# One decoder step on one core: final norm and output by token tile, expert rows gathered raw and scaled afterwards, first slots picked earlier

## The reference, cut to what matters

```python
def _rmsnorm(x, g):
    xf = x.astype(jnp.float32)
    xf = xf * lax.rsqrt(jnp.mean(xf * xf, axis=-1, keepdims=True) + EPS)
    return (xf * g.astype(jnp.float32)).astype(x.dtype)

def _moe(h, w_router, b_router, w_g, w_u, w_d):       # h = _rmsnorm(x, g_ffn)
    logits = (h @ w_router).astype(jnp.float32) + b_router
    probs = jax.nn.softmax(logits, axis=-1)
    topv, topi = lax.top_k(probs, 2)
    topv = topv / jnp.sum(topv, axis=-1, keepdims=True)
    gates = ...                                       # (token, expert), two entries per token
    for e in range(8):
        y = y + gates[..., e:e + 1] * _swiglu(h, w_g[e], w_u[e], w_d[e])
...
x = x + _moe(...)
y = _rmsnorm(x, g_final)
```

## Time and profile before

| | us |
|---|---|
| three runs | 2106.89, 2109.68, 2114.77 (median 2109.68) |
| the profiled execution | 2111.83 |
| its span, first to last instruction | 2110.1 |
| one turn, from transposes to transposes | 75.8 |

### The profile page before, as it was taken

How to read it: one execution, slowest core, us unless ns; L and a number is a source line. 1 busy time by engine, 2 the same in 40 slices (tenths; PEclk the granted TensorE clock), 3 DMA queues, 4 the chain that set the end, 5 groups by cost and what they waited for, 6 DMA issues and landing times.

```text
span 2110.1 us, 35352 instructions
## 1 busy us (share of the span) xinstructions
PE 1886.1 (89%) x14245; PEld 1796.3 (85%) x14245; DVE 1192.0 (56%) x1787; ACT 874.6 (41%) x1305; POOL 186.5 (9%) x226
## 2 busy tenths in 40 slices
PE   4999999877999999969999897877999999999983
PEld 4988987776999999969889787767999999999983
DVE  3765444366333333346654344566787788788872
ACT  5542133614322222155321335244565555555542
POOL 2022200002000000010321000000000000000020
PEclk9999998798999999989999888988999999999995
DMA  4211021014933233222111210235777777778773
GB/s 147 82 51 42 21 72 55 26 64 166 373 94 105 74 96 108 76 55 83 41 41 31 72 45 26 64 109 157 249 265 231 235 262 244 242 248 260 226 219 86
DMA packets 74993, 271.20 MB, mean 129 GB/s; under 512 B 13728, under 2 KB 16176, under 8 KB 72832
## 3 DMA queue, kind: packets, MB, share of 16 engines
q1 hardware_dynamic: 63328, 219.77, 32.9%
q0 software_dynamic: 11552, 49.81, 7.1%
HBM read 234.22 MB, written 35.32 MB: 128 GB/s over the span
## 4 chain that ended last, share of the span: by engine, by line
PE 73%; DVE 14%; ACT 7%; issue 4%; DMA 2%; POOL 1%; DVEq 0%; POOLq 0%; SPq 0%; ACTq 0%
PE ps L633 71%; DVE sb_w_lo L2292 4%; DVE sb_s L1652 2%; ACT sb_s L1165 2%; DVE sb_s L1660 1%; DVE sb_afg L2328 1%; ACT sb_w_hi L1153 1%; ACT L1165 1%; DVE sb_h_lo L1652 1%; DVE sb_w_lo L1643 1%; PE ps L1093 1%; DMA sb_w_raw<-in_wd 1%; PE ps L750 1%; ACT sb_ga L1165 1%; POOL sb_y L491 0%
## 5 line engine op out<-in xcount | busy, mean ns | idle before, releaser
L633 PE MATMUL ps<-sb_h_hi,sb_w_hi 128*128 128x260 f32 x1952 | 578.7, 296 | 31.4 <-DVE sb_h_lo L1652 25.8
L633 PE MATMUL ps<-sb_h_hi,sb_w_lo 128*128 128x260 f32 x1952 | 563.2, 289 | 0.0
L633 PE MATMUL ps<-sb_h_lo,sb_w_hi 128*128 128x260 f32 x1952 | 562.5, 288 | 0.0
L633 PEld LDWEIGHTS ps<-sb_h_hi,sb_w_hi 128*128 128x128 f32 x1952 | 381.0, 195 | 46.6 <-issue 28.3
L1153 ACT ACTIVATE sb_w_hi<-sb_w_raw 128x1024 fp32r<-128x1024 f32 (+2 forms) x144 | 153.9, 1070 | 602.0 <-PE ps L633 601.9
L633 PE MATMUL ps<-sb_hg,sb_w_hi 128*128 128x320 f32 x1408 | 377.9, 353 | 15.3 <-DVE sb_w_lo L2292 8.5
L633 PEld LDWEIGHTS ps<-sb_h_lo,sb_w_hi 128*128 128x128 f32 x1952 | 380.7, 195 | 3.3 <-issue 3.1
L1582 ACT ACTIVATE sb_w_hi<-sb_w_raw 128x1024 fp32r<-128x1024 f32 (+1 forms) x241 | 276.1, 1146 | 251.3 <-PE ps L633 236.5
L633 PEld LDWEIGHTS ps<-sb_h_hi,sb_w_lo 128*128 128x128 f32 x1952 | 380.0, 195 | 0.0
L1643 DVE TENSOR_TENSOR sb_w_lo<-sb_w_raw,sb_w_hi 128x1024 fp32r<-128x1024 f32 (+2 forms) x144 | 181.6, 1262 | 324.6 <-ACT sb_w_hi L1153 324.6
L633 PE MATMUL ps<-sb_hg,sb_w_lo 128*128 128x160 f32 x1408 | 331.9, 236 | 0.0
(11 more groups left out here) (260 smaller groups left out, 2384.5 us busy)
## 6 DMA issues: line engine op xcount, KB each, us to landing
sb_w_raw<-in_wgu SPq DMA_DIRECT2D x223, 512.0 KB, 4.0
sb_w_raw<-in_wd SPq DMA_DIRECT2D x80, 704.0 KB, 6.8
sb_w_raw<-in_wz SPq DMA_DIRECT2D x62, 512.0 KB, 3.5
rows_y<-sb_s POOLq DMA_DIRECT2D x16, 1280.0 KB, 29.7
sb_w_raw<-in_wo SPq DMA_DIRECT2D x16, 384.0 KB, 3.1
rows_y<-sb_x POOLq DMA_DIRECT2D x16, 320.0 KB, 5.5
sb_x<-in_xT SPq DMA_DIRECT2D x8, 260.0 KB, 5.5
rows_h<-sb_rows POOLq DMA_DIRECT2D x5, 416.0 KB, 5.2
```

What stands on the lines that cost most here:

```text
L633: return pe.matmul(out, lhsT, rhs, start=start, stop=stop, skip_group_check=True)
```

## The change

1. Router: `HTK` goes; GpSimd stores the unscaled rows `XTK` to `HX`. `RST` is now Sqrt on ScalarE and a reciprocal on VectorE. Its two parts go into `GE` as two more columns, so that `key` and `slots` also gather the norm factor of each slot, into `GCN[..., 1]`. The last weight split of the output projection moves behind the last `tokens` copy.
2. Turns: `turned` scales the gathered rows first, half s = 0 on ScalarE (80x1024), half s = 1 on VectorE (80x1024); TensorE's transposes wait for both instead of for the gather.
3. First slots: `select(0, 0)`, `key(0)`, `slots(0)` and `fetch(0, 0)` come ahead of the turn count, the register reads and `addresses`.
4. End: one semaphore for each gathered tile of `R2`; add, square with its own sum, square root, reciprocal, scaling of `XTK`, eight transposes and the multiplication by `g_final` run tile by tile, each engine's steps interleaved by program order. `DIAG` and the separate sums go.
5. Some semaphores are merged (`silu_g` and `ssilu_a` into `glu_a` and so on), with their counts moved accordingly.

```diff
@@ pool @@
+            pool.wait_ge(sem["xtk_v"], KT)
             for i in range(NT):
-                pool.wait_ge(sem["htk_a"], i + 1)
-                pool.dma_start(HX[i * TT:(i + 1) * TT, :], HTK[0:TT, i, :])...
+                pool.dma_start(HX[i * TT:(i + 1) * TT, :], XTK[0:TT, i, :])...
...
+            fetch(0, 0)
             pool.wait_ge(sem["turns_v"], 1)
             final = pool.value_load(...)
-            fetch(0, 0)
@@ pe, turned @@
-                pe.wait_ge(sem["hrow_d"], it * 32 + 32)
+                pe.wait_ge(sem["hsc_a"], it + 1)
+                pe.wait_ge(sem["hsc_v"], it + 1)
@@ pe, end @@
-                pe.wait_ge(sem["final_v"], 3 * NT + i + 1)
+                pe.wait_ge(sem["xtk_v"], KT + i + 1)
...
-                    last = mm(PS[...], XTK[0:TT, i, k * P:(k + 1) * P], DIAG[0:TT, i, :])
+                    last = pe.transpose(PS[...], XTK[0:TT, i, k * P:(k + 1) * P], ident[0:TT, 0:TT])
@@ act, router @@
-                ex(RST[0:TT, :], PS[0:TT, 0, 0:NT], ACT.Ln, scale=1.0 / D, bias=EPSC[0:TT, :])
-                own(act, "a_ord")
-                ex(RST[0:TT, :], RST[0:TT, :], ACT.Exp, "rs_a", scale=-0.5)
-                act.wait_ge(sem["xtk_v"], KT)
...
-                    ex(HTK[0:TT, i, :], XTK[0:TT, i, :], ACT.Copy, "htk_a", scale=RST[0:TT, i:i + 1])
...
+                ex(RST[0:TT, :], PS[0:TT, 0, 0:NT], ACT.Sqrt, "rs_a", scale=1.0 / D, bias=EPSC[0:TT, :])
+                act.wait_ge(sem["sel_v"], 1)
+                ex(RTK[:, 4, :, :], RTK[:, 4, :, :], ACT.Exp, "rexp_a")
@@ act, turned @@
+                act.wait_ge(sem["hrow_d"], it * 32 + 32)
+                act.wait_ge(sem["gc_v"], it + 1)
+                ex(HROW[0:ST_, 0, :], HROW[0:ST_, 0, :], ACT.Copy, "hsc_a", scale=GCN[0:ST_, 0, 1:2])
@@ act, end @@
-                inc(act.activation(R2[0:TT, i, :], XTK[0:TT, i, :], ACT.Square), "final_a")
...
+                inc(act.activation(R2[0:TT, i, :], XTK[0:TT, i, :], ACT.Square, accum_out=SS[0:TT, i:i + 1]), "final_a")
+                own(act, "final_a")
+                ex(RST[0:TT, i:i + 1], SS[0:TT, i:i + 1], ACT.Sqrt, "final_a", scale=1.0 / D, bias=EPSC[0:TT, :])
+                if i >= 2:
+                    spread(i - 2)
+            spread(NT - 2)
+            spread(NT - 1)
@@ dve, o2 and order @@
-                if m % OQ == OQ - 1:
+                if m % OQ == OQ - 1 and not (l and m == OU - 1):
                     split_at(UB[l] + ZU + OU + m // OQ + 2)
...
+                        if l and arg == OU:
+                            tokens(OU - 1)
                         sq(2 * l + 1, arg - 1)
                     elif name == "rnf":
                         if l:
-                            tokens(OU - 1)
+                            split_at(UB[l] + ZU + OW + 1)
@@ dve, turned @@
+                dve.wait_ge(sem["hrow_d"], it * 32 + 32)
+                dve.wait_ge(sem["gc_v"], it + 1)
+                ts(HROW[0:ST_, 1, :], HROW[0:ST_, 1, :], GCN[0:ST_, 1, 1:2], ALU.mult, name="hsc_v")
@@ dve, first turn @@
+            select(0, 0)
+            slots(0)
+            turns()
+            addresses()
+            taken(0)
             final = dve.value_load(...)
-            select(0, 0)
-            slots(0)
             turned(0)
@@ dve, end @@
+            def scaled(i):
+                dve.wait_ge(sem["final_a"], 2 * i + 2)
+                inc(dve.reciprocal(RST[0:TT, i:i + 1], RST[0:TT, i:i + 1]), "v_ord")
+                done()
+                ts(XTK[0:TT, i, :], XTK[0:TT, i, :], RST[0:TT, i:i + 1], ALU.mult, name="xtk_v")
...
             for i in range(NT):
-                if i == 0:
-                    dve.wait_ge(sem["r2_d"], 16 * NT)
+                dve.wait_ge(sem[f"r2_d{i}"], 16)
                 dve.wait_ge(sem["final_v"], i + 1)
                 inc(dve.tensor_tensor(XTK[0:TT, i, :], XTK[0:TT, i, :], R2[0:TT, i, :], ALU.add), "final_v")
-            for i in range(NT):
-                sums(i)
...
+                if i >= 1:
+                    scaled(i - 1)
+                if i >= 2:
+                    spread(i - 2)
+            scaled(NT - 1)
+            spread(NT - 2)
+            spread(NT - 1)
```

More of the change, by code:

```diff
@@ L211, in build @@
         new(*[f"w_raw{i}" for i in range(RAW_E)])
-        new("load_x0", "load_x1", "ssum_v", "xtk_p", "xtk_v", "htk_a", "idx_v", "hrow_d", "yrow_a", "ys_d",
-            "beat_g", "final_v", "final_a", "y_stored", "r1_d", "r2_d", "slot_v")
+        new("load_x0", "load_x1", "ssum_v", "xtk_p", "xtk_v", "hsc_a", "hsc_v", "hrow_d", "yrow_a", "ys_d",
+            "beat_g", "final_v", "final_a", "y_stored", "r1_d", "slot_v", "yo_v", "yo_a")
+        new(*[f"r2_d{i}" for i in range(NT)])
         count = dict.fromkeys(sem, 0)
@@ L623, in _ @@
             step(final * 2 + 2)
-            collect(R1, 0, "r1_d")
+            for i in range(NT):
+                collect(R1, 0, i, "r1_d")
             put(final, final * 2 + 3)
@@ L627, in _ @@
             step(final * 2 + 4)
-            collect(R2, 1, "r2_d")
+            for i in range(NT):
+                collect(R2, 1, i, f"r2_d{i}")
         @block.tensor
@@ L740, in l2 @@
                 if i:
[L741 removed]
+                    W(pe, "rs2_a", l, i)
                 else:
@@ L1072, in key @@
                     for i in range(NT):
-                        last = mm(PS[0:ST_, 6, 4 * s:4 * s + 4], SelG[0:TT, i, s * ST_:(s + 1) * ST_], GE[0:TT, i, :],
+                        last = mm(PS[0:ST_, 6, 6 * s:6 * s + 6], SelG[0:TT, i, s * ST_:(s + 1) * ST_], GE[0:TT, i, :],
                                   i == 0, i == NT - 1)
@@ L1303, in l2 @@
                 W(act, "l2_p", l, i + 1)
-                ex(ls[i].rearrange("p (a b) -> p a b", a=4), PS[:, 4:8, 0:HALF], ACT.Ln, "ln2_a", bias=EPSC)
+                ex(ls[i].rearrange("p (a b) -> p a b", a=4), PS[:, 4:8, 0:HALF], ACT.Ln, "rs2_a", bias=EPSC)
                 if i:
-                    own(act, "ln2_a")
+                    own(act, "rs2_a")
                     for i in range(2):
@@ L1482, in sc @@
                                           ACT.Copy)
-                inc(last, "stail_a")
+                inc(last, "tail_a")
             def yhi(l, part):
@@ L1557, in group @@
                         split_next(2 * f)
-                        ex(halves(SG[:, f % 2, :]), slot(1 - f % 2), ACT.Silu, "silu_g")
+                        ex(halves(SG[:, f % 2, :]), slot(1 - f % 2), ACT.Silu, "glu_a")
                         split_next(2 * f + 1)
@@ L1588, in turned, with spread @@
                     ex(HG[:, k, 0, :], PS[:, k // 3, (k % 3) * CAP:(k % 3 + 1) * CAP], ACT.Copy, "hgh_a", scale=par[:, g:g + 1])
+            def spread(i):
+                act.wait_ge(sem["xtk_p"], KT + i + 1)
+                for k in range(4, KT):
+                    a = PAR["g_final"][0] + k
+                    last = act.activation(YO[:, k, i * TT:(i + 1) * TT], PS[:, 2 * (i % 4) + 1, (k % 4) * TT:(k % 4 + 1) * TT],
+                                          ACT.Copy, scale=par[:, a:a + 1])
+                inc(last, "yo_a")
             def rows_out(it):
@@ L1623, in _ @@
                 act.wait_ge(sem["final_v"], NT + i + 1)
-                inc(act.activation(R2[0:TT, i, :], XTK[0:TT, i, :], ACT.Square), "final_a")
[L1625 to L1631, removed]
-                    a = PAR["g_final"][0] + k
-                    last = act.activation(YO[:, k, i * TT:(i + 1) * TT], PS[:, 2 * (i % 4) + 1, (k % 4) * TT:(k % 4 + 1) * TT],
-                                          ACT.Copy, scale=par[:, a:a + 1])
-                inc(last, "final_a")
+                inc(act.activation(R2[0:TT, i, :], XTK[0:TT, i, :], ACT.Square, accum_out=SS[0:TT, i:i + 1]), "final_a")
[5 more added lines that the diff above has]
+            spread(NT - 1)
         @block.vector
@@ L2306, in select, with taken @@
                 cp(GE[0:TT, :, 0:2], g.bitcast(F32), "selg_v")
-                if isinstance(it, int) and it == 0:
-                    addresses()
+                if not (isinstance(it, int) and it == 0):
+                    taken(e)
+            def taken(e):
                 dve.tensor_scalar(expert(KEY[0:TT, :, :], e), expert(KEY[0:TT, :, :], e), float(-CAP), None, ALU.add)
```

123 lines of the change are left out of this document (58 added, 65 removed).

## The result

The changed kernel takes 2132.57 us (median of 4 runs, 2128.96 to 2133.07), the kernel before, timed beside it, 2111.59 us: ratio 1.0093, 95% interval 1.0070 to 1.0116. It is slower by 21.0 us on the medians; the forecast was 2114 us, no change that can be told.

The account below looks back on a forecast made before the run. TensorE, busy 89% of the span, was taken as the bound. End -24.2, router -5.3 and turns +33.4 sum to +3.9 us on the median 2109.7: 2113.6, say 2114 us, range 2101 to 2128.

Parts of the forecast that it names:

- So a turn costs 2.85 + 7/8 x 1.7 = 4.35: Each turn: 2.85 us TensorE stall, plus 1.7 us lost at half clock behind seven of eight gaps.
- The end: Last norm, tile by tile from the first landing, its last spread ending near 2082.1 instead of 2106.3: -24.2 us.
- rival C: At the end, Square and Sqrt need different tables, two loads per tile on ScalarE: total +12.6, 2122 us; chance 0.06.
- The router: Before the first transposes: gather 6.4 us earlier, store late next, less 1.12 us for scaling the rows: -5.3 us.
- The stall of a turn: At m = 2, TensorE waits for VectorE's scaling behind its split of m = 1: 2.85 us with pipe refilling.
- Rival D: In the turns, the scaling never holds TensorE up and costs nothing: total -29.5, 2080 us; chance 0.06.
- rival A: In the turns, the clock holds through the new gaps: turns cost 22.9, total -6.6, 2103 us; chance 0.14.
- The clock's price: In seven turns, work lost at half clock: 1.7 us per 3.4 us stretch, behind seven of eight gaps.
- The last turn: TensorE waits 4.3 us behind a late weight load, but the old 1.99 us gap and half clock are taken up: net 2.9.
- Rival B: In each turn, half clock lasts two stretches, gap and transposes lying in both: turns 48, total +19, 2128 us; chance 0.14.
- the turns: All eight turns' cost from the scaling ahead of the transposes: 7 x 4.35 + 2.9 = +33.4 us.

Follow-up runs that it names:

- the three kernels that had them: Changed kernel (2132.57 us); with only 8 of 1024 columns scaled ahead of the transposes (2123.08 us); with 18 unused products more per turn (2145.75 us).
- the kernel with the longer turn: Changed kernel with 18 unused products more per turn ahead of unit m = 6, far from the gap: 2145.75 us in one run.

## Why the prediction was wrong

**The step that failed** is "So a turn costs 2.85 + 7/8 x 1.7 = 4.35", in its second term. It sized the half clock behind a gap as one stretch of 3.4 us; six of the seven turns that it priced showed two, 6.8 us. These parts around it held:

- The end: -23.7 us for -24.2. The scaling took 0.75 us as taken, eight transposes 1.65 for 1.5, the reading of the square's sum 0.19 for the 0.3 allowed. One table load came, not two per tile, so rival C did not happen.
- The router: -5.2 us for -5.3, with the store as the late strand, as said.
- The stall of a turn: 2.87 us for 2.85, ended by VectorE's scaling behind its split. Rival D did not happen.
- That the clock falls at the gap: in 8 of 8 turns, in four of them while TensorE still waited; rival A did not happen.

The clock's price was 7 x 7/8 x 1.7 = 10.4 us in the forecast. It was 42.9 - 6 x 2.87 - 5.51 = 20.2 us: some 1.6 in turn 0 and 3.1 in each of six turns. The last turn was put at 2.9 us and cost 5.4, 5.51 of gap less the 0.1 by which the tail was shorter. There the wait for ScalarE behind the late weight was 5.51 us where 4.3 were taken, and TensorE then worked for 7.8 us at half clock. That lost 3.9 us, as much as the old gap of 1.99 us and its 3.4 us of half clock had cost (3.7), so the tail gave nothing back. (The 2.9 does not follow from the terms beside it: 4.3 less 1.99 is 2.3.) These two, +9.8 and +2.5, make the turns 45.6 us instead of 33.4, and with the smaller misses (0.5 at the end, 0.1 in the router, 0.4 behind the last spread) the +3.9 becomes +17.1.

Rival B named the right outcome, two stretches: its turns cost 48 us, and 45.6 were measured. That its 2128 us is the time of the profiled execution (2128.96) is partly luck, since that is the lowest of the four runs. Its reason, that the transposes prolong the low clock, did not hold: with a dense unit behind the gap it was the same. And the argument against B, "the stretch seen in the last turn ended after 3.4 us, under dense down units as here", took the price of a gap at another place as the price of this one. The gaps that the prediction went by gave no sign of the other price: each of the seven that it counted, and the one of the last turn, had one stretch of 3.4 us behind it. In the changed kernel the dear outcome repeats itself: with two stretches a turn is 81.6 to 81.9 us long, the falls come 81.9 us apart (1574.11, 1656.03, 1737.95, 1819.87 and on), and so each gap meets the fall much as the last one did. With 18 products more in a turn, the chain broke and every second turn was the cheap one.

The Trainium skill ("TensorE: Matmul & The Clock Gate", section "Why this matters for your kernels") advises against TensorE-idle gaps above about 3 us between bursts of matmuls. The traces differ: gaps of 2.34 and 2.87 us came with half clock in each of turns 0 to 6 of the three kernels that had them, so the measurement decides.

**What stays open**: why the clock stays at half for a second stretch when TensorE was busy throughout the first, as in the turn of 1738 us. The sorting by moment holds for the gap at this place of the turn alone. Elsewhere in the changed kernel a gap of 2.75 us that ended at 1318.4, after the fall at 1318.1, was followed by 3.4 us only; and of the seven gaps in the kernel before, five ended 0.33 us or less before the fall or after it, all with 3.4 us behind them. What the price depends on beside the moment was not tried.

## What to carry to other kernels

A wait on the engine that bounds the kernel costs its length and, where the clock falls at it, as much again: here 2.87 us of wait and up to 3.1 us of half clock in each of seven turns, with 5.4 us in the last, took more than the 29 us that two good edits had won. Put the new work one step ahead of the point where it is needed (or what needs it one step later), and look in the timeline at what stands in front of it on its own engine: moved by one unit, the same scaling was free. And when the price of a clock fall comes from gaps at other places, hold the double of it inside the range.

## What the runs showed of the hardware

- The same gap, at the same instructions, had 3.4 or 6.8 us of half clock behind it, by the moment at which it came (gap of 2.87 us, turns 0 to 6 of the kernel with the longer turn); a gap of 2.34 us was no safer than one of 2.87.
- A loop can lock itself to the dear outcome, or alternate: 81.6 to 81.9 us in turns 1 to 5, or 84.4 and 82.9 us in turn with 18 products more.
- A square whose sum is accumulated carries one instruction more on ScalarE, 0.19 us, and runs behind a Sqrt without another table load.
